# Retention states of a hybrid decoder: eight single steps a head against four steps on strips of the TensorE array

## What is computed

```python
def step(s, inp):
    qc, kc, vc = inp
    scores = jnp.einsum('bihd,bjhd->bhij', qc, kc) * dmask[None]
    inner = jnp.einsum('bhij,bjhe->bihe', scores, vc)
    cross = jnp.einsum('bihd,bhde->bihe', qc, s) * q_dec
    s_new = s * c_dec + jnp.einsum('bjhd,bjhe->bhde', kc * k_dec, vc)
    return s_new, inner + cross
```

## Time and profile before

| | us |
|---|---|
| median of 3 runs | 1679.18 |
| lowest, highest run | 1677.66, 1679.62 |
| span of the profiled execution, first to last instruction | 1674.7 |
| TensorE busy in it | 1625.3 |
| VectorE, ScalarE, GpSimd busy | 853.0, 535.7, 154.8 |

### The profile page before, as it was taken

The page is one execution under the profiler, slowest core; times in us unless marked ns, Lnnn a source line. Parts: engine busy times, 40 slices in busy tenths (PEclk is TensorE's granted clock), DMA queues, the critical chain, the costliest instruction groups (busy, mean ns, idle before and its releaser), DMA issues.

```text
span 1674.7 us, 27448 instructions
## 1 busy us (share of the span) xinstructions
PE 1625.3 (97%) x11258; PEld 1487.3 (89%) x11258; DVE 853.0 (51%) x1042; ACT 535.7 (32%) x829; POOL 154.8 (9%) x147
## 2 busy tenths in 40 slices
PE   7999999999999899999999999989999999999997
PEld 7689879969977799999999999955599999999997
DVE  6457338437635764334434476456656443443343
ACT  4243144225324332212222252136823221222221
POOL 0010001001000330000000040222322000000001
PEclk9999999999999999999999999975999999999999
DMA  6246217226324342222222232200022322232223
GB/s 232 83 158 214 78 63 243 90 69 207 121 63 140 112 153 96 81 93 83 88 88 88 88 101 63 64 8 1 1 68 86 100 87 89 75 100 81 96 76 104
DMA packets 49683, 164.48 MB, mean 98 GB/s; under 512 B 5665, under 2 KB 5729, under 8 KB 49569
## 3 DMA queue, kind: packets, MB, share of 16 engines
q1 hardware_dynamic: 41472, 134.23, 25.2%
q0 software_dynamic: 7408, 26.78, 4.3%
q10 hardware_dynamic: 720, 2.26, 0.3%
HBM read 141.82 MB, written 23.46 MB: 99 GB/s over the span
## 4 chain that ended last, share of the span: by engine, by line
PE 87%; DVE 6%; ACT 3%; issue 2%; DMA 1%; POOL 0%; ACTq 0%; DVEq 0%; SPq 0%; POOLq 0%
PE ps L358 65%; PE ps L372 8%; PE ps L864 2%; PE ps L1138 2%; PE ps L858 2%; DVE arena L1180 2%; PE ps L1160 2%; PE ps L846 1%; PE ps L1149 1%; DVE s_lo L1180 1%; PE ps L876 1%; DVE xg_lo L1186 1%; DVE arena L1278 1%; PE ps L1052 1%; PE ps L1099 1%
## 5 line engine op out<-in xcount | busy, mean ns | idle before, releaser
L358 PE MATMUL ps<-xg_hi,w_hi 128*128 128x272 f32 x1728 | 360.1, 290 | 11.5 <-DVE xg_lo L1186 8.2
L358 PE MATMUL ps<-xg_hi,w_lo 128*128 128x272 f32 x1728 | 358.0, 289 | 0.0
L358 PE MATMUL ps<-xg_lo,w_hi 128*128 128x272 f32 x1728 | 356.8, 288 | 0.0
L341 ACT ACTIVATE w_hi<-w_raw 128x1024 fp32r<-128x1024 f32 x220 | 227.2, 1052 | 374.3 <-PE ps L358 218.4
L346 DVE TENSOR_TENSOR w_lo<-w_raw,w_hi 128x1024 fp32r<-128x1024 f32 x220 | 281.6, 1297 | 63.3 <-ACT w_hi L341 57.7
L358 PE MATMUL ps<-pr_hi,w_hi 128*128 128x272 f32 x1440 | 304.4, 291 | 7.3 <-DVE pr_lo L1180 3.9
L358 PE MATMUL ps<-pr_hi,w_lo 128*128 128x272 f32 x1440 | 301.3, 289 | 0.0
L358 PE MATMUL ps<-pr_lo,w_hi 128*128 128x272 f32 x1440 | 300.3, 288 | 0.0
L358 PEld LDWEIGHTS ps<-xg_hi,w_hi 128*128 128x128 f32 x1728 | 273.3, 189 | 20.8 <-DVE w_lo L346 7.7
L358 PEld LDWEIGHTS ps<-xg_lo,w_hi 128*128 128x128 f32 x1728 | 272.0, 189 | 0.0
L358 PEld LDWEIGHTS ps<-xg_hi,w_lo 128*128 128x128 f32 x1728 | 270.3, 189 | 0.0
(11 more groups left out here) (202 smaller groups left out, 1459.3 us busy)
## 6 DMA issues: line engine op xcount, KB each, us to landing
w_raw<-in_w SPq DMA_DIRECT2D x220, 512.0 KB, 3.6
arena<-in_state SPq DMA_DIRECT2D x32, 512.0 KB, 4.5
out_st_s<-arena POOLq DMA_DIRECT2D x32, 512.0 KB, 4.7
x<-in_x ACTq DMA_DIRECT2D x4, 544.0 KB, 5.8
out_y<-x POOLq DMA_DIRECT2D x8, 272.0 KB, 2.3
out_st_p<-arena SPq DMA_DIRECT2D x4, 512.0 KB, 2.8
arena<-in_dec POOLq DMA_DIRECT2D x4, 256.0 KB, 3.0
arena<-in_cache_v POOLq DMA_DIRECT2D x1, 1024.0 KB, 8.7
```

The costliest lines, as they stand in the source:

```text
L341: nc.scalar.activation(w_hi[:, n.c % 4, :], w_raw[:, n.c % 2, :], ACT.Copy).then_inc(w_hi_done, 1)
L358: last = pe.matmul(ps[:, 2 * bank_pair + s, 0:HT], w_of(w, k), xm[:, k, s * HT:(s + 1) * HT], start=(k == 0 and w == 0 and xi == 0), stop= ...
```

## The change

The eight states of a head become four steps. Step i takes four batches (4q to 4q+3, q = i // 2) at half the depth (d = i % 2): 1 MB. The cross product is taken in plain fp32 straight from the loaded state: four matmuls, each with 32 columns of masked q, each into its own 32 partitions of the PSUM bank. The update is four fp32r matmuls, each over 32 rows of the stacks, each into its own bank (4 to 7). s_hi and s_lo and their passes are gone; q is no longer split, and q_masked is a smaller tile of its own. k and v are stacked so that each strip of 32 rows holds the hi and lo parts of its batch's tokens. There are three places of 1 MB for the four steps; step 3 goes into the place of step 0, behind that step's store. The loads for the next head's steps 0 to 2 are issued later, among the weight blocks behind the gate stage. The step of turn g stands behind product g, none in its middle.

```diff
-UPD_PAIRS = (2, 3)
-QK_PAIRS = (2, 1, 0, 2)
+UPD_BANK = 4
+QK_PAIRS = (0, 1, 2, 0)
...
+STEPS = 4
+S_OFF = (A_STATES, A_STATES + 4 * DV, A_STATE2, A_STATES)
+S_AFTER = (3, 1, 2, 0)
... (SP)
+            def state(one, h, i):
+                q, d = i // 2, i % 2
+                src = A["state"][4 * q:4 * q + 4][:, bass.ds(h, 1)][:, :, d * P:d * P + P].rearrange("b a p e -> (a p) b e")
+                if i == STEPS - 1:
+                    sp.wait_ge(s_out[S_AFTER[i]], (one + 1).times(16).v)
+                elif one.terms or one.c:
+                    sp.wait_ge(s_out[S_AFTER[i]], one.times(16).v)
+                sp.dma_start(s_of(i), src).then_inc(s_in[i], 16)
...
+                    weights(n + (10 + g))
+                    if g == 1:
+                        state(one, h, STEPS - 1)
                 if not last_head:
                     for c in range(8):
                         weights(n + (14 + c))
+                        if c in (2, 4, 6):
+                            state(one + 1, h + 1, c // 2 - 1)
...
-                if n - 4 in range(S_SLOTS):
+                if n - 4 in range(STEPS - 1):
                     state(Index(0), 0, n - 4)
... (ScalarE: state_hi and its calls removed)
+                        rows = k_rep[:, d, :].rearrange("p (r q c t) -> p r q c t", r=4, q=2, c=4)[:, :, q, :, :]
... (TensorE)
+                def state(i):
+                    q, d = i // 2, i % 2
+                    pe.wait_ge(s_in[i], (one + 1).times(16).v)
+                    if i == 0:
+                        pe.wait_ge(o_evac, (one + 1).v)
+                        pe.wait_ge(qm_done, (one + 1).v)
+                    for r in range(4):
+                        at = d * QMW + (4 * q + r) * 32
+                        pe.matmul(ps[32 * r:32 * r + 32, CROSS_BANK, :], q_masked[:, at:at + 32], s_of(i)[:, r, :],
+                                  start=(i == 0), stop=(i == STEPS - 1))
+                    if i == 0:
+                        pe.wait_ge(kmask_done, (one + 1).v)
+                        pe.wait_ge(pstate_evac, (one + 1).v)
+                    else:
+                        pe.wait_ge(s_new, (s_at + i).v)
+                    for r in range(4):
+                        rows = slice(32 * r, 32 * r + 32)
+                        last = pe.matmul(ps[:, UPD_BANK + r, :], k_masked[rows, q, d * P:d * P + P], v_stack[rows, :], start=True, stop=True)
+                    last.then_inc(upd_done, 1)
...
-                    state(2 * g + 1)
+                    state(g)
... (VectorE: state_lo and its calls removed)
+                ch.link(V.tensor_scalar(k_part, k_stack.bitcast(F32), parts_of(1), None, ALU.mult))
+                ch.link(V.scalar_tensor_tensor(out=k_stack, in0=k_st, scalar=parts_of(0), in1=k_part.bitcast(F32), op0=ALU.mult, op1=ALU.subtract))
...
+                def new_state(i):
+                    dve.wait_ge(upd_done, (s_at + i + 1).v)
+                    V.scalar_tensor_tensor(out=s_of(i), in0=s_of(i), scalar=hc(C_G4), in1=ps[:, UPD_BANK:UPD_BANK + 4, :],
+                                           op0=ALU.mult, op1=ALU.add).then_inc(s_new, 1)
...
                     tt(two(gate_t[:, g, :]), pair(GATE_PAIR), two(rstd[:, :]), ALU.mult).then_inc(gate_pre, 1)
-                    if g < 3:
-                        state_lo(2 * g + 2)
-                    new_state(2 * g + 1)
+                    new_state(g)
```

More of the change, by code:

```diff
@@ L93 @@
 DEPTH = len(A_PS)
-QMW = 1056
+QMW = 288
 V_BANKS = (2, 3, 6, 7, 0)
@@ L183, in build @@
         arena = sb("arena", [P, ARENA])
[L185 to L190, removed]
+        spare = pr_hi[:, 4:8, :].rearrange("p k t -> p (k t)")
+        k_masked = spare[:, 0:2 * DK].rearrange("p (q d) -> p q d", q=2)
+        k_stack, k_part = spare[:, 512:512 + DK], spare[:, 768:768 + DK]
+        v_stack, v_part = spare[:, 1024:1024 + DV], spare[:, 1536:1536 + DV]
+        q_masked = sb("q_masked", [P, 2 * QMW])
         q_fac, neg_sink = sb("q_fac", [P, 80]), sb("neg_sink", [P, NG - G_SINK])
@@ L444, in _ @@
                     gp.dma_start(dec, A["dec"][h + 1]).then_inc(dec_in, 16)
[L445 to L448, removed]
+                for i in range(STEPS):
+                    q, d = i // 2, i % 2
+                    gp.wait_ge(s_new, STEPS * h + i + 1)
+                    gp.dma_start(A["st_s"][4 * q:4 * q + 4, h, d * P:d * P + P, :].rearrange("b p e -> p b e"), s_of(i)).then_inc(s_out[i], 16)
                 if h == 0:
@@ L456, in _ @@
             gp.wait_ge(pst_out, 16 * RH)
-            for s in range(S_SLOTS):
-                gp.wait_ge(s_out[s], 16 * RH * B // S_SLOTS)
+            for i in range(STEPS):
+                gp.wait_ge(s_out[i], 16 * RH)
             gp.dma_start(arena[:, A_COSA:A_COSA + 2 * T], A["rope_att"]).then_inc(table_in, 16)
@@ L530, in qk @@
                 for d in range(2):
-                    qv = q_masked[:, d * QMW:(d + 1) * QMW].rearrange("p (b c) -> p b c", c=132)
+                    qv = q_masked[:, d * QMW:(d + 1) * QMW].rearrange("p (b c) -> p b c", c=36)
                     last = nc.scalar.activation(qv[:, :, 0:TD], q_t[:, d, 0:NS_TOK].rearrange("p (b t) -> p b t", t=TD), ACT.Copy)
-                last.then_inc(qhi_done, 1)
+                last.then_inc(qm_done, 1)
                 for d in range(2):
-                    last = nc.scalar.activation(k_rep[:, d, :].rearrange("p (r t) -> p r t", r=4),
-                                                k_t[:, d, 0:NS_TOK].unsqueeze(1).broadcast_to([P, 4, NS_TOK]), ACT.Copy)
+                    for q in range(2):
+                        rows = k_rep[:, d, :].rearrange("p (r q c t) -> p r q c t", r=4, q=2, c=4)[:, :, q, :, :]
+                        src = k_t[:, d, 16 * q:16 * q + 16].rearrange("p (r t) -> p r t", t=TD).unsqueeze(2).broadcast_to([P, 4, 4, TD])
+                        last = nc.scalar.activation(rows, src, ACT.Copy)
                 last.then_inc(krep_done, 1)
             def head(one, last_head):
-                n, s_at = one.times(RET_BLOCKS) + RET_FIRST, one.times(B)
+                n, s_at = one.times(RET_BLOCKS) + RET_FIRST, one.times(STEPS)
                 parts = O_PARTS[last_head]
@@ L556, in head @@
                 act.wait_ge(vrep_mm, (one + 1).v)
-                nc.scalar.activation(v_stack[:, :], ps[:, VREP_BANK, :], ACT.Copy).then_inc(vhi_done, 1)
+                nc.scalar.activation(v_stack, ps[:, VREP_BANK, :], ACT.Copy).then_inc(vhi_done, 1)
                 split_hi(act, n + 7)
[L560 to L566, removed]
                 act.wait_ge(pstate_mm, (one + 1).v)
@@ L910, in before @@
                     if c == 2:
[L911 removed]
+                        pe.wait_ge(s_new, (s_at + STEPS).v)
                 def beside(c, k):
                     if (c, k) == (1, 1):
[L916 removed]
+                        pe.wait_ge(s_new, (s_at + STEPS).v)
                         pe.wait_ge(cross_evac, (one + 1).v)
```

105 lines of the change are left out of this document (34 added, 71 removed).

## The result

The changed kernel takes 1650.78 us (median of 4 executions, 1645.97 to 1657.31) against 1678.73 us (4 executions, 1677.66 to 1679.62): a ratio of 0.9853, 95% interval 0.9808 to 0.9899. Of the 28 us some 20 to 23 belong to the change.

The account below looks back on a forecast made before the run. TensorE, busy in 97% of the span, was taken as the bound. Gate stages were to save 16.6 us, less 1.1 us of delays elsewhere: 15.5 us off 1679.2 us, rounded to 1664 us, range 1655 to 1684.

Parts of the forecast that it names:

- Forecast A: Gate stage: row and column strips run side by side; 1664 us, own range 1656 to 1670, chance 0.48.
- S: TensorE's time for one gate-stage step, four cross and four update matmuls with changes of tile shape; forecast 1.9 us.
- Rival B: Cross product: a strip's second record holds back the next strip's first; S 2.9 us, about 1678.5 us, chance 0.19.
- Rival C: Cross product: column strips don't overlap at all; S 4.7 us, a stretch 43.8 us, about 1707 us, chance 0.19.
- Rival D: Gate stage: step 3's load is the bound, 2 to 4 us late a head; 1671 to 1679 us, chance 0.10.
- floor of issue: Within a step on TensorE: least time between issued records, 0.24 / 4 = 0.06 us, taken from 32-column records.
- The stretch: One head's gate stage on TensorE: products 24.1, variance matmul 0.9 and four steps, 32.6 us without waits, 32.9 with the load.
- The 0.3 us a head for the fourth load: Gate stage: allowance for step 3's 1 MB load, which was early or up to 4.3 us late.
- The last stretch: Last head's gate stage up to the first matmul behind it, with 2.9 us for the last new state: 35.8 against 39.00.
- The 0.6 us for VectorE's tail behind the gates: Heads 0 to 2: last new state ends 2.7 us into the next q product, mixing follows; 0.2 us a head taken.
- The start cost: Kernel start: three 1 MB loads among the first weight blocks delay them by 0 to 4.5 us, 0.5 taken.
- the 4.5 us between the profiled span and the median: Whole kernel: median of the runs shown over the 1674.7 us span, left as it is, giving 1679.2 as starting time.

Follow-up runs that it names:

- e1: The changed kernel with all four cross matmuls of a step on the first 32 partitions instead of four strips: 1689.13 us, ratio 1.0113 to the kernel before.
- e3: The changed kernel with its 1 MB state loads issued later, at the start and between heads: 1645.26 us, ratio 0.9841 to the kernel before.

## Why the prediction was right and wrong

**The direction and the mechanism were right.** Forecast A was that strips run side by side on rows and columns, S from 1.4 to 2.3 us, and S is 1.63. The evidence for row strips did carry over to column strips, although these read four moving operands from the same partitions. Rival B, the staircase, falls by the four records in the first 0.06 us of a step and by 0.99 us where it needs 5 x 0.436. Rival C, no overlap, falls with e1, which is what C describes: its 43.8 us a stage against 41.6 measured, and 27 us slower than before against 17 to 21 (its S of 4.7 had the update serial too). The place from which C decides, S above 3.1, is borne out in kind: e1's S is 4.2 and it is slower. Rival D, the late load, shows as 0.4 us in one head of four.

**Two terms failed.** S was mis-sized (4.3 us), and TensorE's clock, which had no term at all, makes 5 to 8 of the 28 us; it is the clock that put the time outside the range.

**S was mis-sized by its floor of issue.** I read 0.06 us between records from four 32-column records and charged it nine times, 0.54 us. Four strips start within 0.04 us of each other: the cross product with its change of shape is 0.09 + 0.99 = 1.08 us where 1.33 was put down, the update 0.44 for 0.51. The rows of another form were no price for records that stand on other strips. Sixteen times 0.27 is 4.3 us. The estimate worked from the figures of the Trainium skill (TensorE: Matmul & The Clock Gate, "Part 3: Packing small matmuls — row/col tiling") was 1.7, nearer, but by luck, since its errors offset each other: columns are better than it had them (3.56 / 0.99 = 3.6 times for four), row strips worse (1.01 / 0.44 = 2.3 in place of 3.07). The same section of the Trainium skill has matmuls start in strict program order. If both records of a matmul stand together in the program, as rival B took, the trace of column strips does not agree, with four strips' first records ahead of any second; the trace does not number the records.

**The stretch.** With S = 1.63 the prediction's own sum is 24.1 + 0.9 + 6.5 = 31.5 us; measured 31.4, 31.85 and 31.35. So the products, the variance matmul and the step add up, and the waits that were counted as gone are gone. The 0.3 us a head for the fourth load was 0.4 in one: its 1 MB lands in 6.8 us (median), between the bounds of 4.5 and 9.0, inside the 8.3 us. The last stretch, 34.3 for 35.8, differs by the same terms; its wait of 2.85 us and the new state's 2.35 us (2.5 put down) are as forecast. The stages gave 22.2 us where 16.6 were counted: 4.3 from S, 0.8 from the load, 0.5 from the rest.

**Costs elsewhere.** The 0.6 us for VectorE's tail behind the gates did not show (101.35 us between heads 2 and 3 for 101.2). The start cost 0 to 2 us: the first gate stage begins at 92.5 and 93.8 us in the two profiles of before, at 93.7, 94.4 and 93.8 after, and 0.5 was taken. The place I had not costed is the loop-back to head 2, 3.3 us against the first profile of before. I had moved SP's loads in my working and asked only who waits for the data; that TensorE could wait longer for its own program was not among the rivals. It is smaller than 3.3 as a cost of the change: in the second profile of before TensorE waits 2.6 us there, not 2.2, and the stretch to the next gate stage is 2.0 us longer than in its first; e3 wins back some 2 us.

**The rest of the miss is the clock, a term put at nothing.** Retention is 17.7 us shorter in the first pair of profiles and 20.1 in the second (603.0 to 582.9), against 15.5 forecast. The other part of the 28 us is which clock the executions had: those shown before the prediction lay at 1677.7 to 1679.6, where the kernel before has its lower group (median 1677.8); of the four of the change two lay in the higher group. At the lower clock the change takes 1657.3 us, inside A's own 1656 to 1670. The three runs shown agreed within 2 us, and the prediction took 3.4 us for what can be told from no change; over 58 executions the kernel before spreads over 22. The prediction had no term for that: it took the 4.5 us between the profiled span and the median as time around the span, whereas an execution is 2.1 us longer than its own span (1.9 after), and the rest of the 4.5 lay in other executions than the profiled one. The clock column of the windows was read only in the gate stages, where it is 1.00; the attention stage stands at 0.88 in that same profile, and executions that differ there by 0.05 differ by 11 us (279.6 - 268.2).

## What to carry to other kernels

Small matmuls over one depth but on four column strips run as one, plain fp32 too, with 0.1 us for each change of tile shape: ask of a tile of 32 columns what could stand on the other 96. Before shortening a piece of work on the bounding engine further, look for what it covers; here it is VectorE's read of the only pair of banks, and below about 1 us a step wins nothing. And before forecasting a few tenths of a per cent, look at the granted clock of every stage of the profile, not only of the one that changes: a stage below full clock is a term of the range.

## What the runs showed of the hardware

Four plain fp32 matmuls of 512 columns on four column strips take 0.99 us, on one strip 3.56; the first records of all four strips are in flight within 0.04 us, before any second record. Four fp32r matmuls of 32 rows on four row strips take 0.44 us, against 1.01 for 128 rows. A change of tile shape costs 0.09 to 0.11 us. Behind the loop-back to head 2, TensorE's first matmul started 1.7 us after a 16 KB packet of the instruction queue had landed, in all nine profiles. Behind waits of TensorE of 2.6 and 3.6 us there the granted clock was 0.50, the lower of its two levels (1.2 and 2.4 GHz), over the next 2.0 us, and behind one of 2.2 us it stayed at 1.00; behind the loop-back to head 1 it fell to 0.51 after 2.27 us in one run and stayed at 1.00 after 2.60 us in another. One and the same stage of attention ran at a mean granted clock of 0.88, 0.90 or 0.93, in 279.6, 276.1 and 268.2 us; what decides between these is open.
